# Order of TensorE's work in the state-space scan: both quarters of the first column half between the two cores

## What is computed

```python
o_a = (attn * jax.nn.silu(z_a)) @ w_o_attn
o_b = y @ w_o_ssd
merged = jax.nn.sigmoid(g_a) * o_a + jax.nn.sigmoid(g_b) * o_b
x = x + (merged @ w_out).astype(x.dtype)
```

## Time and profile before

| | |
|---|---|
| median of three runs | 2196.99 us |
| the profiled execution | 2199.09 us |
| its span | 2197.4 us |
| TensorE matmul busy | 2097.8 us, 95% |
| VectorE busy | 1648.0 us, 75% |
| ScalarE busy | 1211.5 us, 55% |
| GpSimd busy | 473.1 us, 22% |
| mean granted TensorE clock | 0.976 |

### The profile page before, as it was taken

One profiled execution on the slowest core, in us unless ns is written; L12 is line 12 of the kernel. 1 busy time (PEld: TensorE's weight loads), 2 busy tenths in 40 slices (PEclk: granted clock), 3 DMA queues, 4 the chain that ended last, 5 costly groups with the idle time before them and its releaser, 6 DMA issues. The chain is left out here.

```text
span 2197.4 us, 38495 instructions
## 1 busy us (share of the span) xinstructions
PE 2097.8 (95%) x13003; PEld 1894.5 (86%) x13003; DVE 1648.0 (75%) x2896; ACT 1211.5 (55%) x2599; POOL 473.1 (22%) x490
## 2 busy tenths in 40 slices
PE   5999999999999999999999699999968999997999
PEld 3999999999999999999999588878746778876887
DVE  6878887787888778889965656556457889985665
ACT  6446665644666565476654555556455676643231
POOL 1000000000000000000000455555435677860000
PEclk8999999999999999999999699999978999998999
DMA  6334443344444334334543444444446667655442
GB/s 125 117 118 142 143 163 121 130 130 130 143 143 156 117 130 143 118 130 143 163 137 129 137 109 114 108 114 118 123 151 177 181 188 215 198 157 174 132 146 92
DMA packets 336208, 307.84 MB, mean 140 GB/s; under 512 B 69289, under 2 KB 296433, under 8 KB 336049
## 3 DMA queue, kind: packets, MB, share of 16 engines
q1 hardware_dynamic: 336065, 305.98, 45.3%
HBM read 216.22 MB, written 89.73 MB: 139 GB/s over the span
## 5 line engine op out<-in xcount | busy, mean ns | idle before, releaser
L1067 PE MATMUL x_ps<-hh,wh 128*128 128x352 f32 x1008 | 328.3, 326 | 7.2 <-DVE hl L825 5.5
L1069 PE MATMUL x_ps<-hh,wl 128*128 128x352 f32 x1008 | 324.5, 322 | 0.0
L1068 PE MATMUL x_ps<-hl,wh 128*128 128x352 f32 x1008 | 324.2, 322 | 0.0
L552 ACT ACTIVATE wh<-w_raw 128x512 fp32r<-128x512 f32 x336 | 210.3, 628 | 141.6 <-PE z_ps L1069 80.7
L801 DVE TENSOR_TENSOR wl<-ws,wh 128x512 fp32r<-128x512 f32 x252 | 171.4, 689 | 109.4 <-ACT wh L552 109.2
L801 DVE TENSOR_TENSOR wl<-w_raw,wh 128x512 fp32r<-128x512 f32 x336 | 229.8, 684 | 5.1 <-ACT wh L552 0.2
L581 ACT ACTIVATE arena<-x_ps 128x352 f32<-128x352 f32 x252 | 116.6, 463 | 204.7 <-PE x_ps L1069 204.5
L1067 PE MATMUL z_ps<-hh,wh 128*128 128x352 f32 x672 | 219.2, 326 | 0.0
L1069 PE MATMUL z_ps<-hh,wl 128*128 128x352 f32 x672 | 215.7, 321 | 0.0
L1068 PE MATMUL z_ps<-hl,wh 128*128 128x352 f32 x672 | 215.5, 321 | 0.0
L1067 PEld LDWEIGHTS x_ps<-hh,wh 128*128 128x128 f32 x1008 | 189.9, 188 | 16.0 <-issue 16.0
(11 more groups left out here) (294 smaller groups left out, 5555.7 us busy)
## 6 DMA issues: line engine op xcount, KB each, us to landing
w_raw<-in_w_in_dram SPq DMA_DIRECT2D x84, 1024.0 KB, 5.2
proj<-row SPq DMA_DIRECT2D x84, 704.0 KB, 3.3
arena<-acs_dram SPq DMA_DIRECT2D x16, 1024.0 KB, 7.5
arena<-proj SPq DMA_DIRECT2D x8, 1280.0 KB, 9.0
s_feat<-proj SPq DMA_DIRECT2D x8, 1280.0 KB, 7.6
a_z<-proj SPq DMA_DIRECT2D x16, 512.0 KB, 4.4
a_gate_t<-proj SPq DMA_DIRECT2D x16, 512.0 KB, 4.2
branch_rows<-a_branch SPq DMA_DIRECT2D x16, 512.0 KB, 3.2
```

What stands on the lines that cost most here:

```text
L552: act.activation(wh[:, j], left(n, j), ACT.Copy).then_inc(whi_ready, 1)
L1067: pe.matmul(out, wh[:, j, k], hh[:, j, k], start=first and k == 0, stop=False, skip_group_check=more)
L1068: pe.matmul(out, wh[:, j, k], hl[:, j, k], start=False, stop=False, skip_group_check=more)
L1069: mm = pe.matmul(out, wl[:, j, k], hh[:, j, k], start=False, stop=k == 3, skip_group_check=more)
```

## The change

Only the order of TensorE's pieces in a step of the scan changes. No instruction is added or taken away, no semaphore changes, and the other engines' programs stay as they are.

```diff
@@ -2568,9 +2568,10 @@
                     if has_prev(m):
                         fn(m - 1, 1 - slot, *a)
 
+                prev(gates, 0)
                 core(m, slot, 0)
-                prev(gates, 0)
                 prev(run, 0, 0)
+                prev(run, 0, 1)
                 if has_prev(m):
                     squares(m - 1)
                 core(m, slot, 1)
@@ -2578,10 +2579,9 @@
                     products(m + 1, 1 - slot)
                 if has_next(m):
                     x_rows(m + 1, 1 - slot, 0)
-                prev(run, 0, 1)
+                prev(run, 1, 0)
                 if has_next(m):
                     x_rows(m + 1, 1 - slot, 1)
-                prev(run, 1, 0)
                 prev(gates, 1)
                 prev(run, 1, 1)
```

## The result

| | before | after |
|---|---|---|
| median | 2197.47 us (2196.13 to 2198.72, 4 runs) | 2232.41 us (2232.06 to 2233.11, 4 runs) |
| profiled execution | 2199.09 us | 2233.11 us |
| its span | 2197.4 us | 2231.4 us |
| mean granted TensorE clock | 0.976 | 0.979 |

The ratio is 1.0158, with a 95% interval of 1.0146 to 1.0170. The changed kernel is 34.9 us slower; the forecast was 2229 us, 32 slower.

What follows compares the result with a forecast made beforehand. TensorE set the scan's 19.87 us step, VectorE 1.5 us behind; the change closes a 22.44 us loop. Fourteen periods add 32.1 us, other terms 0: 2231.2 profiled, 2229 us median, range 2214 to 2244.

Steps and rivals of the forecast that it cites:

- The loop: Scan step, L2395 of merge(m - 2, 1) through quarter 0 1, core 1, VectorE to next L2395: period 22.44 us, +2.57.
- TensorE's own path: Scan step: TensorE's path alone, including the wait for L2395 of merge(m - 1, 0), would already give 21.77 us.
- The waits of 1.8 and 0.7 us: TensorE idle twice per step waiting for L2395: 1.8 us before quarter 1 1, 0.7 before the next quarter 0 1.
- The place of gates 0: Gates 0 ahead of core 0 start core 0 some 0.36 us later in the step; price on TensorE 0.
- the other queues: GpSimd, ScalarE and SyncE behind the waiting quarter: later work still fits the longer step, cost nothing.
- The joints: New adjoining TensorE pieces in a scan step: taken as 0, a tenth of a us either way.
- The sum: Step 2 to step 16: thirteen periods of 22.44 plus 22.97, 314.7 against 282.6 us, +32.1 us.
- Step 1: Quarter 0 1 moves into a place where TensorE idled anyway: taken as 0, bounds -1 and +3 us.
- The clock: Rival: two idle times per step lower TensorE's clock to 0.70 over the whole scan, 2301 us; 6%.
- VectorE did not get faster: Rival denied here: VectorE operations L2323, L2374, L2399 shorten, step bound by TensorE again, 2193 us; 3%.
- ScalarE's late decays: Rival, ScalarE late as before ahead of L2323: its 6.9 us on top give 2236 us, inside the range.
- The reading by which it fits as it stands: Rival: quarter 0 1, wanted 5.90 us after core 0 starts, has L2395 at 5.91; no change, 2197 us; 3%.

Runs made afterwards that it cites:

- the run that relieved the first loop: Changed kernel with VectorE's merge(m - 2, 1) moved ahead of inter(m, 0): 2221.78 us, ratio 1.0109.
- gates 0 alone: Kernel before with one edit, gates 0 moved ahead of core 0: 2197.69 us, ratio 1.0000.
- both merges and the load early: Changed kernel with merge(m - 2, 1) ahead of inter(m, 0), merge(m - 1, 0) ahead of masked(m + 1), decays' load ahead of SyncE's store: 2199.62 us.

## Why the prediction was right, point by point

**The loop.** 4.53 + 17.91 = 22.44 us was forecast; 4.52 + 17.87 is in the trace, and the steps repeat at 22.4. That these terms form the loop is shown by the runs: taking quarter 0 1 out from between L2395 and core 1 brought the old time back, 0.43 us added there came out as 0.43 us per step, and with the quarter left there the time fell only as VectorE's part of the circle was made shorter, and even then, with the load early as well, the circle still set 20.1 us.

**The second, TensorE's own path.** 21.77 us was forecast, 21.5 stands in the run that relieved the first loop. It is not TensorE's path alone: 8.13 us of it are VectorE's, from core 1 to L2395 of `merge(m - 1, 0)`, so it is a second loop. The waits of 1.8 and 0.7 us were seen as 1.49 and 0.58. The forecast counts from where the next piece could have started, the profile from the end of the record ahead: gates 1 start at 1922.09, quarter 1 1 could follow 0.36 us later and starts at 1924.18, which is 1.73.

**Prices of 0.** The place of gates 0 costs nothing (1.0000 alone; the same 1.0158 with and without it). Nor do the other queues cost anything from step 2 on: the periods stay at 22.4 us although ScalarE waits for its load and quarter 1 0 three times for ScalarE. The joints were priced at 0, and the period of 19.86 with gates 0 first bears that out; with two quarters adjoining and x_rows 1 next to gates 1 as well it is 19.80, a gain of 0.07 us per step on TensorE, inside the tenth that was allowed.

**The sum.** From step 2 to step 16: 314.7 forecast, 313.99 measured. Step 1: 0 with bounds of -1 and +3. From the first core 0 of the scan to that of step 2 it is 63.1 us in the profile before and 63.9 in the one after. Over all profiles, the five kernels with quarter 0 1 behind core 1 take 61.9 to 63.1 us there, 62.2 on average, and the six with it ahead of core 1 take 62.8 to 63.9, 63.6 on average. So that term is about 1.4 us, inside its bounds, and 0 was too low. In the changed kernel TensorE waits there 3.49 us for the last low weights (L2311) and 2.25 us for ScalarE: I had looked at the room on TensorE and not at the inputs of the quarters.

**What was off.** The sum was about 3 us short: 32.1 forecast, 34.9 between the medians, with 32.1 as the low end of the interval. The mechanism stands; of the terms, the 14 periods came out 0.7 us smaller (31.4), and step 1, taken as 0, was mis-sized by 1.4. Behind step 16 the pair of profiles shows 0.6 less, but from core 0 of step 16 to the end all profiles scatter by more (233.2 to 236.0 us in the five kernels, 234.4 to 236.9 in the six). Taken as they stand, the three make 32.2, at the edge of the interval.

A part of the rest lies in the one profile of the kernel before, from which the sum was read. Its start is the earliest of all eleven, but its step 1 is long (63.1 us, against 61.9 to 62.0 in the four other kernels with quarter 0 1 behind core 1), and it has three late steps. The kernel with gates 0 alone has two, and takes 281.7 us from core 0 of step 2 to that of step 16 where this profile takes 282.6 and the changed kernel 314.3. Against that kernel the 14 periods cost 32.6 us, and with 1.4 for step 1 the estimate is 34.0. Each kernel has one profile only, so whether the last us has a cause in the change stays open.

**The rivals.** The clock did not fall: 1.00 from step 2 to step 16, with gaps of 0.58 and 1.49 us in every step. By the rule of the Trainium skill, page "TensorE: Matmul & The Clock Gate", section "A second HAM failure mode: psum-queue depth-cycling", short idle times between groups of matmuls could have made it swing; no run here shows that at these gaps. VectorE did not get faster: L2323, L2374 and L2399 take 1.14, 1.15 and 1.22 us in the step shown, as before, and its work per step is 18.40 us. ScalarE's late decays, 6.9 us for VectorE's L2323 in the kernel before, are no longer among VectorE's waits from step 2 on: the changed kernel has no late step there. That the longer steps give the load more time is likely and was not tested.

The reading by which it fits as it stands (5.91 against 5.90 us) held for step 2 alone, as the prediction said of it. There quarter 0 1 starts with no wait booked, right behind the end of L2395; in step 3 the wait is there:

```profile
1686.85 0.74 DVE L2395 SCALAR_TENSOR_TENSOR s_rows<-s_o_ps,s_stat,s_rows 128x512 f32<-128x512 f32 x1
```

```profile
1687.74 0.47 PE L74 MATMUL s_o_ps<-s_w_hi,s_y_hi 128*128 128x512 f32 x1
...
1710.10 0.47 PE L74 MATMUL s_o_ps<-s_w_hi,s_y_hi 128*128 128x512 f32 x1 [0.60 <-DVE s_rows L2395]
```

The reading is right about one step and blind to the fact that the same quarter, by standing ahead of core 1, delays the very L2395 that it waits for in the next.

**Attribution.** I had looked for VectorE's 3 us of idle time as a wait for `i_ps`. It is 3.1 us, but 2.27 of it is booked on L2405, which waits for the squares. The squares had moved behind the quarter too.

## What to carry to other kernels

Before work is moved ahead of a step's release, follow the released engine around to what the moved work waits for: if it closes a circle, the sum around the circle is the new period, and a wait that "just fits" in the old trace tells of the first step only. A filler belongs where neither its start nor its end is on such a circle: moving the same four transpositions between two places changed nothing, and at a third they cost 0.43 us a step more. When one loop is relieved, the next can be close behind (here 22.4, then 21.5, then a late load, then 20.1 from the first loop again), so work out the second before promising the first one's price. And a circle is open only when nothing leads back around it; moving a piece along it makes it shorter.

## What was not expected of the hardware

When a float32 quarter's first matmul follows the 128 x 512 matmul of core 0 directly, its record starts 0.4 us earlier than that of the transpositions did, but lasts 0.79 us instead of 0.48. So at this joint the start of the record does not tell when the quarter advances; what adds up is the distance between the later records. Since records overlap, a short wait can also be missing from the list of waits: with both merges and the load early, quarter 0 1 was held up by about 0.27 us in a step, and nothing was booked, since the record ahead lasts 0.39 us where the next one usually starts 0.23 us behind it.
